# Attention projections with weights and rows loaded in the stage ahead, and head norm weights spread on chip

## The reference, cut to what matters

```
shift, scale, gate = split(silu(c) @ ada_w[0] + ada_b[0], 3)      # and the same with c_ctx
h = rms_norm(x, norm_w[0]) * (1 + scale) + shift                  # x: latents, and ctx for the context
q_a, k_a, v_a, c_q, c_kv, k_pe, gate = split_cols(h @ w_in, ...)   # w_in: 1024 x 2208
q_a = rms_norm(q_a per head, q_norm_w);  k_a = rms_norm(k_a per head, k_norm_w)
q_m  = rms_norm(c_q, cq_norm_w) @ w_uq                             # 256 -> 8 heads x 96
kv_m = rms_norm(c_kv, ckv_norm_w) @ w_ukv                          # 128 -> 8 heads x 128
# then rotary embedding; of the context only keys and values are used
```

## Time and profile before

| | |
|---|---|
| median of 3 runs | 4913.47 us (4912.9 to 4920.15) |
| profiled execution, its own time | 4910.12 us |
| its span | 4908.1 us |
| TensorE busy in the span | 4173.6 us, mean granted clock 0.927 |
| stage 1 ends, stage 2 begins | 91.20 us |
| stage 3 begins | 174.32 us |

### The profile page before, as it was taken

The page is one execution under the profiler, slowest core; times in us unless marked ns, Lnnn a source line. Parts: engine busy times, 40 slices in busy tenths (PEclk is TensorE's granted clock), DMA queues, the critical chain, the costliest instruction groups (busy, mean ns, idle before and its releaser), DMA issues. The chain is left out here.

```text
span 4908.1 us, 59293 instructions
## 1 busy us (share of the span) xinstructions
PE 4173.6 (85%) x20947; PEld 2139.3 (44%) x20947; DVE 1898.4 (39%) x2965; ACT 1097.4 (22%) x1816; POOL 258.2 (5%) x366
## 2 busy tenths in 40 slices
PE   3699699998999998999679997786999599949995
PEld 0355355555444445777534444442333244413331
DVE  1233345443322113898734936532111333321112
ACT  0122255443110012222111135310000234100000
POOL 0000000000000000110100000000000200000001
PEclk7799899999999998999889999997999799969998
DMA  7322221112365511111161112135865511266666
GB/s 258 117 68 63 60 49 38 37 36 84 139 218 210 200 64 56 42 39 52 43 211 35 43 54 102 53 104 232 321 264 214 187 31 49 100 265 228 251 235 261
DMA packets 260939, 627.18 MB, mean 128 GB/s; under 512 B 73549, under 2 KB 153501, under 8 KB 240969
## 3 DMA queue, kind: packets, MB, share of 16 engines
q1 hardware_dynamic: 221906, 508.13, 29.3%
q0 software_dynamic: 19424, 94.01, 5.1%
q10 hardware_dynamic: 19480, 23.31, 1.3%
HBM read 1298.29 MB, written 113.53 MB: 288 GB/s over the span
## 5 line engine op out<-in xcount | busy, mean ns | idle before, releaser
L1645 PE MATMUL hyp_acc<-hy_hT,hyp_early_weights 128*128 128x512 f32 x768 | 335.9, 596 | 0.0
L3423 PE MATMUL blocks_h<-moe_w,blocks_xT 128*32 128x512 f32 x2560 | 291.1, 607 | 42.3 <-issue 42.3
L3423 PE MATMUL blocks_h<-od_hT,blocks_xT 128*32 128x512 f32 x1280 | 290.9, 608 | 25.7 <-DMA moe_w1b<-in_ex_w 20.6
L3444 PE MATMUL blocks_acc<-moe_w,blocks_hidT 128*32 128x512 f32 x2560 | 284.5, 596 | 11.2 <-DMA moe_w<-in_ex_w 9.9
L3423 PE MATMUL blocks_h<-moe_w1b,blocks_xT 128*32 128x512 f32 x1280 | 290.8, 608 | 0.0
L970 PE MATMUL att_scores<-att_kT,att_qT 64*128 64x512 f32 (+3 forms) x768 | 252.2, 549 | 22.7 <-DMA att_v<-scratch_V 22.7
L700 PE MATMUL lat_acc<-lat_w_in,lat_hT 128*128 128x512 f32 (+1 forms) x640 | 244.6, 538 | 2.2 <-DMA lat_w_in<-in_attn_w_in 2.2
L2209 PE MATMUL evp_acc<-ev_hT,evp_early_weights 128*128 128x512 f32 x512 | 224.6, 600 | 7.6 <-DVE evp_qkT L2350 5.6
L906 DVE TENSOR_REDUCE att_nmax<-att_scores 128x1 f32<-128x1280 f32 x128 | 190.2, 1486 | 102.2 <-PE att_scores L970 102.2
L994 PE MATMUL att_turn<-ident,att_probs 128*128 128x128 f32 x1280 | 192.5, 281 | 42.3 <-DVE att_o L936 22.5
L1645 PEld LDWEIGHTS hyp_acc<-hy_hT,hyp_early_weights 128*128 128x128 f32 x768 | 145.1, 191 | 174.3 <-issue 174.2
(11 more groups left out here) (520 smaller groups left out, 6067.5 us busy)
## 6 DMA issues: line engine op xcount, KB each, us to landing
moe_w<-in_ex_w SPq DMA_DIRECT2D x320, 2048.0 KB
od_hT<-in_ex_w SPq DMA_DIRECT2D x80, 2048.0 KB
moe_w1b<-in_ex_w SPq DMA_DIRECT2D x80, 2048.0 KB
hyp_m_weights<-in_mod_w POOLq DMA_DIRECT2D x6, 8192.0 KB, 24.2
mod_weights<-in_ada_w SPq DMA_DIRECT2D x6, 4096.0 KB, 22.7
scratch_y_rows<-blocks_x ACTq DMA_DIRECT2D x40, 512.0 KB, 8.9
hyp_early_weights<-in_hy_w_in SPq DMA_DIRECT2D x8, 2048.0 KB
scratch_parts<-hyp_uT SPq DMA_DIRECT2D x24, 512.0 KB, 3.7
```

Source lines behind the costliest of these rows:

```text
L1645: mm = nc.tensor.matmul(acc[:, m % 2, half * NC:(half + 1) * NC], weights[:, ws, kt, c:c + P], hT[:, kt, half * NC:(half + 1) * NC], start ...
L3423: mm = nc.tensor.matmul(out[mine, :], xT[:, kt, mine], w[l][:, kt, :], start=(kt == 0), stop=(kt == KT - 1))
L3444: mm = nc.tensor.matmul(acc[mine, c, :], hidT[:, kt, mine], w2[l][:, kt, c * NC:(c + 1) * NC], start=(kt == 0), stop=(kt == FT - 1))
```

## The change

`w_kv`, `w_ukv`, the context's x tiles, the norm row and the head norm weights are loaded by SP at the end of stage 1, behind the third group's weights, and are kept for both projections. What only the latents need (`w_q`, the gate's weights, `w_uq`, x, all three rows) is loaded by SP in stage 2. The head norm weights come as one row of 512 numbers on one partition; a matmul with a row of ones spreads them into PSUM, and VectorE copies them out. In stage 1 the weights of a group come in two halves of four row blocks each with a semaphore of its own, and the bias rows have a semaphore of their own and are issued behind the weights.

```
+class Projection:      # w_kv, w_ukv, x, col_rows, w_row [1, 512], one [1, 128] and their semaphores
+class Queries:         # w_q, w_gate, w_uq, x, col_rows and their semaphores
+def load_projection(sp, d, early):
+    for s in range(2):
+        sp.dma_start(early.x[:, s, :], d["ctx"][0][s * P:(s + 1) * P, :]).then_inc(early.x_in[s], 16)
+    sp.dma_start(early.col_rows[2 * KT:, :], d["norm_w"][0].rearrange("(kt p) -> kt p", p=P)).then_inc(early.cols_in, 16)
+    at = 0
+    for v, n in (("attn_q_norm", HD), ("attn_k_norm", HD), ("mla_q_norm", MQR), ("mla_kv_norm", MKR)):
+        sp.dma_start(early.w_row[:, at:at + n], d[v][0].rearrange("(a n) -> a n", a=1)).then_inc(early.heads_in, 16)
+        at += n
+    wv = d["attn_w_in"][0].rearrange("(kt p) n -> p kt n", p=P)
+    for c, (a, b) in enumerate(KV_CHUNKS):
+        sp.dma_start(early.w_kv[:, :, a - C_K:b - C_K], wv[:, :, a:b]).then_inc(early.kv_in[c], 16)
+    sp.dma_start(early.w_ukv[:, :], d["mla_w_ukv"][0]).then_inc(early.ukv_in, 16)
+def load_queries(sp, d, early):
+    load_rows(sp, d, early, 0)
+    sp.dma_start(early.col_rows[2 * KT:, :], d["norm_w"][0].rearrange("(kt p) -> kt p", p=P)).then_inc(early.cols_in, 16)
+    for s in range(2):
+        sp.dma_start(early.x[:, s, :], d["x"][0][s * P:(s + 1) * P, :]).then_inc(early.x_in[s], 16)
+    wv = d["attn_w_in"][0].rearrange("(kt p) n -> p kt n", p=P)
+    for c, (a, b) in enumerate(Q_CHUNKS):
+        to = early.w_q[:, :, :] if c == 0 else early.w_gate[:, :, a - C_GATE:b - C_GATE]
+        sp.dma_start(to, wv[:, :, a:b]).then_inc(early.q_in[c], 16)
+    sp.dma_start(early.w_uq[:, :, :], d["mla_w_uq"][0].rearrange("(kt p) n -> p kt n", p=P)).then_inc(early.uq_in, 16)
+def load_rows(sp, d, early, vec):
+    for n, v in enumerate((d["mods"][vec, 0:D], d["mods"][vec, D:2 * D])):
+        sp.dma_start(early.col_rows[n * KT:(n + 1) * KT, :], v.rearrange("(kt p) -> kt p", p=P)).then_inc(early.cols_in, 16)
...
 def stage_modulations(nc, d, svec, early):
@@ SP
+                    for h in range(2):
+                        kts = slice(h * KT // 2, (h + 1) * KT // 2)
+                        for j in range(0, Q, 2):
+                            layer, c = divmod(g * Q + j, per)
+                            two = slice(c * NC, (c + 2) * NC)
+                            sp.dma_start(weights[:, s, kts, j * NC:(j + 2) * NC],
+                                         d["ada_w"][layer].rearrange("(p kt) n -> p kt n", kt=KT)[:, kts, two])\
+                                .then_inc(w_in[s][h], 16)
                     for j in range(Q):
...
-                        sp.dma_start(bias[32 * j:32 * (j + 1), s, :], row(d["ada_b"][layer, chunk], 32)).then_inc(w_in[s], 16)
+                        sp.dma_start(bias[32 * j:32 * (j + 1), s, :], row(d["ada_b"][layer, chunk], 32)).then_inc(bias_in[s], 16)
                     if g == 0:
                         load_filter()
+                load_projection(sp, d, early)
@@ TensorE
-                    pe.wait_ge(w_in[s], signals(24 * Q * (g // S + 1)))
                     if g >= S:
                         pe.wait_ge(summed, signals(g - S + 1))
-                    modulate_group(nc, acc[:, s, :], svec, weights[:, s, :, :]).then_inc(product, 1)
+                    for h in range(2):
+                        pe.wait_ge(w_in[s][h], signals(32 * (g // S + 1)))
+                        mm = modulate_group(nc, acc[:, s, :], svec, weights[:, s, :, :], range(h * KT // 2, (h + 1) * KT // 2))
+                    mm.then_inc(product, 1)
...
 def attention_project(nc, tag, d, ident, src, n_tiles, key0, vec, with_queries, early, queries):
@@ SP
-                load_x(0, 0)
-                ...
-                    sp.dma_start(w_uq[:, :, :], d["mla_w_uq"][0].rearrange("(kt p) n -> p kt n", p=P)).then_inc(w_ups_in, 16)
+                if not with_queries:
+                    load_rows(sp, d, early, vec)
                 for s in range(S):
                     load_rope(0, s)
+                if not with_queries:
+                    load_queries(sp, d, queries)
@@ GpSimd
+                nc.gpsimd.memset(one[:, :], 1.0).then_inc(consts, 1)
-                pool.wait_ge(consts, signals(6))
+                pool.wait_ge(consts, signals(7))
@@ ScalarE: the four broadcasts are gone
@@ VectorE
-                    dve.wait_ge(heads_in, signals(16 * 4))
-                    nc.vector.tensor_scalar(w_head[:, 0:GQ, :], w_head[:, 0:GQ, :], HD ** -0.5, None,
-                                            ALU.mult).then_inc(prepared, 1)
+                    dve.wait_ge(rows_spread, signals(1))
+                    nc.vector.tensor_scalar(w_head[:, 0:GQ, :], up[:, 1, 0:HD].unsqueeze(1).to_broadcast([P, GQ, HD]),
+                                            HD ** -0.5, None, ALU.mult)
+                    nc.vector.tensor_copy(w_head[:, GQ:, :], up[:, 1, HD:2 * HD].unsqueeze(1).to_broadcast([P, GKV, HD]))
+                    nc.vector.tensor_copy(w_low[:, :], up[:, 1, 2 * HD:NC]).then_inc(prepared, 1)
@@ TensorE
                 nc.tensor.transpose(up[:, 0, 0:3 * KT], col_rows[:, :], ident[0:3 * KT, 0:3 * KT]).then_inc(cols_turned, 1)
+                pe.wait_ge(heads_in, signals(16 * 4))
+                pe.wait_ge(consts, signals(7))
+                nc.tensor.matmul(up[:, 1, :], one[:, :], w_row[:, :], start=True, stop=True).then_inc(rows_spread, 1)
```

More of the change, by code:

```diff
@@ L140, with __init__ @@
 HY_EMB = 1 + 2 * HY_BANDS
-def stage_modulations(nc, d, svec):
+class Projection:
+    def __init__(self, nc, ctx):
+        sb, _, sem, _ = tools(nc, ctx, "proj_early")
+        self.w_kv, self.w_ukv = sb("w_kv", [P, KT, C_GATE - C_K]), sb("w_ukv", [P, MH * (NOPE + HD)])
+        self.x, self.col_rows = sb("x", [P, 2, D]), sb("col_rows", [3 * KT, P])
+        self.w_row, self.one = sb("w_row", [1, NC]), sb("one", [1, P])
+        self.cols_in, self.heads_in, self.ukv_in = sem("cols_in"), sem("heads_in"), sem("ukv_in")
+        self.kv_in = [sem(f"kv_in{c}") for c in range(2)]
+        self.x_in = [sem(f"x_in{s}") for s in range(2)]
+        self.sems = [self.cols_in, self.heads_in, self.ukv_in] + self.kv_in + self.x_in
@@ L266, in _, with modulate_group @@
                         reduce_arguments(g)
-def modulate_group(nc, acc, svec, weights):
-    for kt in range(KT):
+def modulate_group(nc, acc, svec, weights, kts=range(KT)):
+    for kt in kts:
         for j in range(MODS_AT_ONCE):
@@ L368, in schedule, with weights @@
             finish(last, 1)
-        begin()
+        def weights(kt, a, b):
+            if C_K <= a and b <= C_GATE:
+                return early.w_kv[:, kt, a - C_K:b - C_K]
+            return queries.w_q[:, kt, a:b] if b <= QA else queries.w_gate[:, kt, a - C_GATE:b - C_GATE]
+        begin(() if with_queries else queries.sems)
         with nc.Block() as block:
@@ L699, in project @@
                     for kt in range(KT):
[L700 removed]
+                        mm = nc.tensor.matmul(acc[:, (s * NCH + c) % 2, 0:b - a], hT[:, s, kt, :], weights(kt, a, b),
                                               start=(kt == 0), stop=(kt == KT - 1))
```

79 lines of the change are left out of this document (39 added, 40 removed).

## The result

The kernel with the change took 4876.16 us (median of 4 runs, 4869.02 to 4881.52), the kernel before beside it 4914.01 us (4 runs, 4912.9 to 4920.15). The ratio is 0.992, 95% interval 0.9904 to 0.9936: faster by 37.9 us, where 4873.6 us (39.9 less) was forecast. The profiled execution took 4874.79 us, its span is 4873.0 us.

The account below looks back on a forecast made before the run. The prediction took TensorE to bound the kernel, busy 4173.6 of 4908.1 us. Terms -0.7 - 19.2 - 20.0 = -39.9 us took 4910.1 to 4870.2 us profiled, 4873.6 as a median; range 4866 to 4887.

Parts of the forecast that it names:

- 1. End of the modulations: Modulations' end: TensorE done 3.4 us earlier by halves, stores landing 2.7 us later beside the prefetch; net -0.7 us.
- rival A: Modulation stores and two row loads land only after the prefetch backlog: +2.0 us, then 2 us less gain; 4878; chance 0.14.
- 2. Context head: Context projection's head, stage start to first projection matmul, falls from 27.2 to 8.0 us; gain 19.2 us.
- DVE's three operations are free: Context stage: three head-weight operations, 1 to 1.5 us together, fall in DVE's idle time and cost nothing.
- the loads for the latents are hidden: Context stage: 8.13 MB for the latents, 20.1 us on SP, end 17 us before the stage's first store.
- The rest of the stage waits on no load and stays: Context stage after its first projection matmul, 118.37 to 174.32 us before: no change in length.
- Rival C: Whole kernel: shifted stages lower TensorE's mean clock from 0.927 to 0.916, adding 50 us; 4924; chance 0.02.
- 3. Latent head: Latent projection's head falls from 28.0 to 8.0 us with nothing loaded before it; gain 20.0 us.
- Rival B: The trickle belongs to the small row loads and moves with them into the prefetch; net -10 us, 4903; chance 0.03.
- Rival D: Stores land as on a free queue and the clock rises earlier at both heads: -5 us more, 4868; chance 0.11.

Follow-up runs that it names:

- e6: The changed kernel with TensorE waiting for both weight halves of a group before its first matmul; median 4881.53 us, ratio 0.9924 to the kernel before.
- e8: The changed kernel with GpSimd's clear of the head buffer moved behind the first tile's row scale; median 4879.63 us, ratio 0.9918 to the kernel before.
- e10: As e9, but x's first tile, the rows and the first w_kv chunk (2.6 MB) prefetched in the modulations; median 4869.40 us, ratio 0.9905 to the kernel before.
- e5: The kernel before with only the two wider broadcasts left and ones for the q and k head weights; 4900.01 us, one run.
- e11: The kernel before with broadcasts on SP's queue behind the head's loads and VectorE's wait for them behind the second tile's xn; median 4894.37 us.
- e2: The changed kernel with the four broadcasts back on ScalarE's queue and no spreading matmul; median 4887.95 us, ratio 0.9937 to the kernel before.
- e9: The changed kernel with w_kv and w_ukv loaded in the context stage and the head buffer's clear behind VectorE's first xn; median 4874.10 us, ratio 0.992.
- e3: The kernel before with the four broadcasts moved to SP's queue, after the rope rows; 4911.86 us, ratio 0.9989.
- e1: The kernel before with one-row loads and the spreading matmul in place of the four broadcasts, no prefetch, no halves; median 4881.62 us, ratio 0.9925.
- e4: The kernel before with the four broadcasts replaced by loads of the same shapes from distinct addresses; 4902.63 us, one run.
- e0: The changed kernel measured once more, unaltered; median 4878.63 us, ratio 0.9924 to the kernel before.

## Why the prediction was right, step by step

The forecast of 4873.6 us is 2.6 us off the median of 4876.16, and at the attention's start 38.7 us were gained where the sum said 39.9.

**1. End of the modulations, forecast -0.7, measured -1.3** (91.20 to 89.86). Both of its terms were larger. The halves brought the first store 4.5 us forward (87.04 to 82.55), not 3.4: the 32 matmuls took 5.32 us, the lower of the two values, not 6.1. The landing beside the backlog cost 3.15 us (7.31 less 4.16), not 2.7. What I had not seen is that they are one thing: the stores' packets start only as the backlog runs out, and by e6 the stage begins at about the same time whatever the halves do. So the forecast's mechanism was wrong here, a landing beside the backlog at a price of 2.7 us, and rival A's is the true one; that the term came out only 0.6 us off was luck. Rival A's price was wrong, since it added a landing of 4.3 us to the prefetch's end at 87.4 us. The end was about right (the rate falls just past 86, the last load lands at 88.1 us), but the stores' packets start at 86.2 and end at 87.4 us, and the stage follows at 89.86. The rule of the Trainium skill that was weighed there (DMA: Bandwidth & Descriptors, queues, rings and completion order: each engine takes turns between its queues, packet by packet) is not borne out by these runs for four stores of 6 KB: with 4.3 MB on the other queue they came through only as it ran out (7.3 us to the stage), with 1.1 or 2.6 MB, which end ahead of them, in 4.2.

**2. Context head, forecast 27.2 to 8.0, measured 8.3.** The row loads were there after 2.7 us (2.4 forecast). The spread took 2.05 us, not 1.7, and ended 0.6 us behind xn, not 0.3. Gain 18.9 of 19.2. That DVE's three operations are free held: 0.68 + 0.28 + 0.55 = 1.5 us, in an idle time until the second tile's xn at 110.74. That the loads for the latents are hidden held too: they ended about 118 us, the stage's first store was issued at 133.76.

"The rest of the stage waits on no load and stays" failed by 2.6 us. It still waits on no load; but its matmuls run at 1.2 GHz for longer (the groups above). In both kernels the clock rises during the 16 matmuls of the first chunk and falls after them. Before, it stood at 1.00 from 122 to 132 us and fell behind the second tile's transposes. After, it stood at 1.00 from 104 to 110 us, was at 0.76 from 110 to 111 and at 0.50 from 111 on: it fell in the idle time just ahead of the transposes, and rose again only between 116 and 118. The length of the head does not decide which of the two happens. In e8 and e10 (heads of 8.4 and 7.4 us, bodies of 56.1), in e5 (12.5, body 54.3) and in e11 (10.6) these transposes take 1.09 to 1.10 us as before; in e2, with a head of 20.0 us, they take 1.97 and the body 58.1. What decides it isn't settled here. Rival C had the mechanism, a clock that falls at another place once the stages shift, and was right in sign at this one place, with 2.6 us where it needed 40.

**3. Latent head, forecast 28.0 to 8.0, measured 8.1.** Gain 19.9 of 20.0. Next late is, as forecast, GpSimd's memset: e9, which moves it away, has 6.2 us. The latent body gained 1.2 us that were not forecast (349.0 to 347.8), within what the same code scatters here: 347.2 to 349.7 in all kernels but e3 and e11.

**The sum:** 1.3 + 18.9 - 2.6 + 19.9 + 1.2 = 38.7 us.

**Rival B** (the trickle is the small row loads', and moves with them) is out: with five of them in the prefetch no stretch at 20 GB/s is left; e1, with all its row loads inside the stage, has the column rows 4.6 us after the stage's start; and e4 and e5 put the trickle on the broadcasts. The rule that spoke for it, the Trainium skill's price of a small descriptor (DMA: Bandwidth & Descriptors, why small descriptors are slow: 27% at 256 bytes), is neither confirmed nor refuted in size by e4, whose four loads landed in 4.5 to 6.2 us beside other loads; it does not describe a load in which every run reads one address. **Rival D** had neither of its terms: the stores were later than forecast, not earlier, and in the context stage the first chunk's 16 matmuls took 9.85 us where they had taken 8.86, so the clock rose later there and not earlier.

What the prediction got from the profile and what from luck: the two large terms came from the rows of the trickle. The small ones, -0.7 and 0, were off by -0.6 and +2.6, opposite in sign; that they nearly made up for each other, with scatter on top, was luck. The range has a slip: its own terms (-34, 3 for the clock, 6.7 for the scatter) add up to 4889 at the top, not 4887; the result lies far inside either.

## What to carry to other kernels

When a load of a few KB takes 15 us, look at the rate of the stretch before its own queue: a busy share of 0.08 at 20 GB/s means that something else trickles, and here a broadcast from one row of HBM to 128 partitions did, at 15 ns a packet. Load the row once and spread it with a matmul against ones; that alone gave 31.8 of 38.7 us. Size a prefetch to end before the stores that the next stage waits for: with the 2.6 MB that the first matmuls need (e10) the stage began 2.8 us earlier than with 4.3 MB (e0), and its head was no longer.

## What the runs showed of the hardware

- Loads that spread one row of HBM over partitions: 1536 packets in 23.4 us at 20 GB/s, with the other queue's 2 MB loads held for most of it. The same packets from distinct addresses landed in 4.8 us instead of 16.8. Whether memory or the making of the packets lets them go so slowly, and why that holds the other queue, was not tried.
- Small stores on ScalarE's queue moved only as SP's backlog of loads ran out: first packet 3.6 us after the issue against 0.7 us without a backlog, 7.3 us from issue to the next stage against 4.2 us, and with the issue 3.4 us later still the same stage start (89.86 and 90.21).
- VectorE's 128x1024 operation beside a GpSimd memset of 2.18 us took 2.58 us instead of 0.75 (e8), and 0.75 again when the two were kept apart (e9). The Trainium skill (SBUF — State Buffer, on who interferes with whom) says that `tensor_scalar` on VectorE can enter a mode that uses a port pair shared with GpSimd, that whoever issues first keeps the pair for the whole instruction, and that the other is blocked. The runs agree: the memset started first, and xn ended 0.55 us after it.
- The same eight transposes after the same wait of 3.5 us took 1.10 us at 2.4 GHz in some kernels and 1.97 us at 1.2 GHz in others. In the kernel after, with the groups beside them, that made 2.6 us in a body of 55.9 us. What decides when the clock falls was not found.
